# Conditioning units of a fused two-block kernel moved behind the expert loop, with a new order in its router stage

## What is computed

```python
def ada_modulation(c, w, b):
    m = jax.nn.silu(c) @ w + b                       # [1024] @ [1024, 3072]
    shift, scale, gate = jnp.split(m[:, None, :], 3, axis=-1)
    return shift, scale, 1.0 + gate

def moe_ffn(h, w_router, b_router, w_gate_up, b_gate_up, w_down, b_down):
    logits = hf @ w_router + b_router                # top 4 of 32 experts
    ...                                              # rows of a token's experts
        gu = xb @ w_gate_up[e] + b_gate_up[e]        # 1024 -> 2048
        glu = gate * jax.nn.sigmoid(SWIGLU_ALPHA * gate)
        return ((up + 1.0) * glu) @ w_down[e] + b_down[e]

def second_block(x, c, ...):
    for layer in range(2):
        shift, scale, gate = ada_modulation(c, ada_w[layer, 0], ada_b[layer, 0])
        y = mixer_ab(x * (1.0 + scale) + shift, ...)   # layer 0; mixer_c in layer 1
        x = layer_norm(DN_ALPHA * x + gate * y, ...)
        shift, scale, gate = ada_modulation(c, ada_w[layer, 1], ada_b[layer, 1])
        y = squared_relu_mlp(x * (1.0 + scale) + shift, ...)
        x = layer_norm(DN_ALPHA * x + gate * y, ...)
```

## Time and profile before

| | us |
|---|---|
| median of 3 runs | 1933.98 (1928.10 to 1935.94) |
| profiled execution | 1928.87, span 1927.0 |
| TensorE busy | 1826.0 (95%), mean granted clock 0.977 |
| DVE busy | 694.6 (36%) |
| ACT busy | 539.6 (28%) |
| input projection of the mixer starts | 89.14 |
| output projection of the mixer starts | 171.80 |
| logits done | 294.17 |
| first expert's bias matmuls start | 323.96 |
| last expert's down matmuls end | 1260.92 |
| scores of the ab attention start | 1328.72 |

### The profile page before, as it was taken

The page is one execution under the profiler, slowest core; times in us unless marked ns, Lnnn a source line. Parts: engine busy times, 40 slices in busy tenths (PEclk is TensorE's granted clock), DMA queues, the critical chain, the costliest instruction groups (busy, mean ns, idle before and its releaser), DMA issues.

```text
span 1927.0 us, 24801 instructions
## 1 busy us (share of the span) xinstructions
PE 1826.0 (95%) x10198; PEld 1129.0 (59%) x10198; DVE 694.6 (36%) x1177; ACT 539.6 (28%) x714; POOL 34.3 (2%) x21
## 2 busy tenths in 40 slices
PE   6999989999999999999999999996899999989997
PEld 6785764443434434434434434464589987769996
DVE  3243322111111111111111111158865568676545
ACT  4342431101111111111111111045634454464442
POOL 0100120000000000000000000000000000000001
PEclk9998998999999999999999999997799999999999
DMA  9758599999999999999999999913144553424550
GB/s 337 285 197 329 187 380 398 428 428 429 428 428 429 429 429 428 429 428 429 428 428 429 429 429 428 418 59 119 32 165 175 190 213 142 175 103 143 202 197 34
DMA packets 96315, 587.14 MB, mean 305 GB/s; under 512 B 6990, under 2 KB 7204, under 8 KB 70660
## 3 DMA queue, kind: packets, MB, share of 16 engines
q1 hardware_dynamic: 94820, 581.25, 74.6%
q10 hardware_dynamic: 1440, 5.11, 0.8%
HBM read 585.30 MB, written 1.05 MB: 304 GB/s over the span
## 4 chain that ended last, share of the span: by engine, by line
PE 88%; DVE 4%; ACT 4%; DMA 3%; issue 1%; SPq 0%; DVEq 0%; ACTq 0%
PE bank L1063 34%; PE bank L1319 23%; PE bank L1338 12%; PE bank L1276 7%; PE bank L1348 3%; PE bank L1310 2%; DMA ring<-in_ada_w 1%; PE bank L1138 1%; ACT arena L811 1%; PE bank L1331 1%; PE bank L1123 1%; ACT sb_XN L896 1%; DMA ring<-in_w_o 1%; PE bank L1255 0%; DMA ring<-in_w_in 0%
## 5 line engine op out<-in xcount | busy, mean ns | idle before, releaser
L1319 PE MATMUL bank<-ring,arena 128*64 128x512 f32 x2048 | 454.7, 596 | 0.0
L1319 PEld LDWEIGHTS bank<-ring,arena 128*64 128x64 f32 x2048 | 141.6, 137 | 307.4 <-issue 307.4
L1063 PE MATMUL bank<-w_hi,arena_r 128*128 128x512 f32 (+1 forms) x784 | 258.0, 391 | 4.7 <-DVE arena_r L2027 2.8
L1338 PE MATMUL bank<-ring,arena 128*64 128x512 f32 x1024 | 226.8, 595 | 16.8 <-ACT arena L811 16.8
L502 DVE TENSOR_TENSOR w_lo<-ring,w_hi 128x4096 fp32r<-128x4096 f32 (+2 forms) x45 | 196.5, 4367 | 47.3 <-ACT w_hi L492 44.9
L1063 PEld LDWEIGHTS bank<-w_hi,arena_r 128*128 128x128 f32 x784 | 148.0, 189 | 35.4 <-DVE arena_r L2027 3.3
L492 ACT ACTIVATE w_hi<-ring 128x4096 fp32r<-128x4096 f32 (+2 forms) x45 | 158.9, 3574 | 34.9 <-DMA ring<-in_c_w_in 19.2
L809 ACT ACTIVATE arena<-arena,sb_tab 128x512 f32<-128x512 f32 x32 | 23.1, 722 | 510.5 <-DVE arena L1930 510.5
L1338 PEld LDWEIGHTS bank<-ring,arena 128*64 128x64 f32 x1024 | 72.5, 137 | 150.5 <-issue 144.9
L1905 DVE TENSOR_SCALAR arena<-sb_tab,sb_pos 128x64 f32<-128x64 f32 x66 | 13.8, 252 | 387.7 <-PE bank L1319 387.7
L1063 PE MATMUL bank<-XT_r,w_hi 128*128 128x256 f32 x512 | 145.8, 285 | 4.3 <-DVE arena_r L2148 4.3
(11 more groups left out here) (341 smaller groups left out, 2120.3 us busy)
## 6 DMA issues: line engine op xcount, KB each, us to landing
ring<-in_w_gate_up SPq DMA_DIRECT2D x128, 2048.0 KB, 14.4
ring<-in_w_down SPq DMA_DIRECT2D x64, 2048.0 KB, 16.7
ring<-in_mlp_w SPq DMA_DIRECT2D x32, 2048.0 KB, 8.3
ring<-in_ada_w SPq DMA_DIRECT2D x24, 2048.0 KB, 12.5
ring<-in_c_w_in SPq DMA_DIRECT2D x6, 2048.0 KB, 7.6
ring<-in_w_in SPq DMA_DIRECT2D x4, 2048.0 KB, 10.0
ring<-in_w_k SPq DMA_DIRECT2D x2, 2048.0 KB, 12.2
ring<-in_w_v SPq DMA_DIRECT2D x2, 2048.0 KB, 9.1
```

Source lines behind the costliest of these rows:

```text
L1063: mm = pe.matmul(out, st[a], mv[b], start=start and a + b == 0, stop=stop and a == 1, skip_group_check=True)
L1319: mm = pe.matmul(B[m][CAP * h:CAP * h + CAP, :], xe[:, 2 * j + kl, :], w[:, kl, m * D + h * HW:m * D + (h + 1) * HW], start=False, stop=(j ...
L1338: mm = pe.matmul(B[2][CAP * h:CAP * h + CAP, :], hT[:, c, CAP * j:CAP * j + CAP], w[:, c, h * HW:(h + 1) * HW], start=(j == 0 and c == 0), ...
```

## The change

The first three sublayers' conditioning (18 units) stays ahead of the experts: 2, 4, 2, 1, 5 and 4 units in the six places, for 2, 3, 6, 1, 5 and 7. The six units of the fourth sublayer (`late`) come through `POST` as three granules of two transfers each, between ab_in 2 and ab_out 0, with the query weights behind the first. TensorE does two of them in place of the five `keep_busy` matmuls, one between two groups of transposes, three in the first steps of the ab attention, where their combines go too. The split of ab_out 1 moves from ahead of aqT's copy into the attention. In the router stage the first gather stands ahead of the table, and DVE does `gains_xe` ahead of it. In the loop the last eighth of the gather comes behind `hidden_T`. DVE writes the normalised rows in a reordered layout, so that the gather reads contiguous columns. POOL makes the fourth sublayer's gains from the late result.

```diff
-ADA_AT = [("k", 2, (0, 1), 2), ("v", 3, (0, 1), 2), ("mix", 6, (4, 5, 4, 5, 4, 3), 2), ("q", 1, (4,), 6), ("scores", 5, (5, 4), 6),
-          ("router", 7, (1, 2), 4)]
+LATE = 18
+ADA_AT = [("k", 2, (0, 1), 2), ("v", 4, (0, 1), 2), ("mix", 2, (4, 3), 2), ("q", 1, (4,), 6), ("scores", 5, (5, 4), 6),
+          ("router", 4, (1, 2), 4)]
...
-AHEAD = {("ada", 18): (0, 1), ("ada", 20): (2, 3)}
+AHEAD = {("ada", 15): (0, 1), ("ada", 17): (2, 3)}
...
-POST = ([("ab_in", i) for i in range(3)] + [("uq", 0)] + [("ab_out", i) for i in range(2)] + [("mlp0", i) for i in range(16)]
+POST = ([("ab_in", i) for i in range(3)] + [("late", 0), ("uq", 0), ("late", 1), ("late", 2)]
+        + [("ab_out", i) for i in range(2)] + [("mlp0", i) for i in range(16)]
...
+        def late_part(u):
+
+            if u in (LATE, LATE + 3, LATE + 5):
+                return [vec[:].rearrange("p a n -> p (a n)"), wr[:].rearrange("p k n -> p (k n)")]
+            at = 1224 if u == LATE + 4 else 9216
+            return [arn(at, S), arn(at + S, S)]
...
+            if name == "late":
+                out = []
+                for s2, u in ((s, LATE + 2 * i), (HI_SLOTS[POST_SLOTS.index(s)], LATE + 2 * i + 1)):
+                    w = A["ada_w_2"][u // 12, u // 6 % 2].rearrange("(k p) n -> p k n", p=P)
+                    out.append((slot(s2).rearrange("p (k n) -> p k n", k=8), w[:, :, HW * (u % 6):HW * (u % 6) + HW]))
+                return out
...
                 sp.wait_ge(used, NPRE if OWNER[g] is None else OWNER[g] + 1)
+                if name == "late" and g < MOE_END + R2:
+                    sp.wait_ge(used, MOE_END)
...
+            last = mod[:, 3, :]
+            pool.wait_ge(sem("late_read"), 2)
+            pool.tensor_tensor(last, last, ada_bT[:, 72:96], ALU.add).then_inc(sem("late_mod"), 1)
...
+            def late(u, b):
+
+                n = u - LATE
+                if n % 2:
+                    act.wait_ge(*done("late", n // 2))
+                else:
+                    act.wait_ge(sem("late_mm"), n // 2 + 1)
+                for i, part in enumerate(late_part(u)):
+                    act.activation(part, B[b][:, i * S:(i + 1) * S], ACT.Copy).then_inc(sem("late_part"), 1)
...
                 for u in range(units):
+                    if st == "ab" and u < 3:
+                        if u == 2:
+                            act.wait_ge(sem("late_comb"), 4)
+                        late(LATE + 3 + u, 7)
+                    if st == "ab" and u == 1:
+                        split_hi(act, "ab_out", 1)
...
+            late(LATE, 7)
+            late(LATE + 1, 6)
+            act.wait_ge(sem("late_comb"), 2)
+            act.activation(mod[:, 3, 0:8], B[7][:, 0:8], ACT.Copy).then_inc(sem("late_read"), 1)
             split_hi(act, "ab_out", 0)
-            split_hi(act, "ab_out", 1)
...
+            late(LATE + 2, 2)
             act.wait_ge(sem("ab_T"), 5)
...
-            def gather():
+            def gather(a=0, b=KC):
 
-                for k in range(KC):
+                for k in range(a, b):
                     for t in range(TB):
-                        rows = XN[:, t, 2 * P * (k // 2):2 * P * (k // 2 + 1)].rearrange("p (q r) -> p r q", r=2)
-                        mm = pe.matmul(B[3][:, k * CAP:(k + 1) * CAP], rows[:, k % 2, :], sel_tok[:, t, :],
+                        mm = pe.matmul(B[3][:, k * CAP:(k + 1) * CAP], XN[:, t, k * P:(k + 1) * P], sel_tok[:, t, :],
                                        start=(t == 0), stop=(t == 1))
-                mm.then_inc(sem("e_gather"), 1)
+                if b == KC:
+                    mm.then_inc(sem("e_gather"), 1)
 
-            ada(2)
+            ada(1)
...
-            ada(2)
+            ada(1)
+            pe.wait_ge(*upto("ffn", "xn", 2))
+            pe.wait_ge(sem("e_sel"), 2)
+            gather()
             pe.wait_ge(sem("flag"), 1)
...
-            pe.wait_ge(*upto("ffn", "xn", 2))
-            pe.wait_ge(sem("e_sel"), 2)
-            gather()
-            ada(1)
             ada_flush()
...
                 pe.wait_ge(sem("e_sel"), i * (2 * E_BLOCK) + (2 * n + 4))
-                gather()
+                gather(0, KC - 1)
                 pe.wait_ge(sem("e_h"), i * E_BLOCK + (n + 1))
                 hidden_T()
+                gather(KC - 1)
...
+            def late_step(u):
+
+                if u == 1:
+                    late_raw.extend(late_granule())
+                if u:
+                    pe.wait_ge(*upto("ab", "pte", 2 * u))
+                late_combine(LATE + 2 + u, 5, 400 + 4 * u)
+                if u < 3:
+                    late_main(LATE + 3 + u, late_raw[u], 7)
...
                         scores(st, u + 2, q, k)
+                    if st == "ab" and u < 4:
+                        late_step(u)
                     pe.wait_ge(*upto(st, "p", 2 * u + 2))
...
+            def late_main(u, raw, b):
+
+                w = raw.rearrange("p (k n) -> p k n", k=KC)
+                for r in range(2):
+                    for c in range(4):
+                        mm = pe.matmul(B[b][32 * c:32 * c + 32, :], cs[:, 2 * c + r, :], w[:, 2 * c + r, :],
+                                       start=(r == 0), stop=(r == 1))
+                mm.then_inc(used if (u - LATE) % 2 else sem("late_mm"), 1)
+
+            def late_combine(u, b, at_col):
+
+                pe.wait_ge(sem("late_part"), 2 * (u - LATE) + 2)
+                for i, part in enumerate(late_part(u)):
+                    for c in range(2):
+                        col_at = at_col + 2 * i + c
+                        mm = pe.matmul(B[b][:, col_at:col_at + 1], part[:, c * P:(c + 1) * P], quads[:, 0:1],
+                                       start=True, stop=True)
+                mm.then_inc(sem("late_comb"), 1)
...
-            keep_busy(7, 5)
+            late0 = late_granule()
+            late_main(LATE, late0[0], 7)
+            late_main(LATE + 1, late0[1], 6)
+            pe.wait_ge(sem("late_part"), 4)
...
             mm.then_inc(sem("ab_T"), 1)
+            late_combine(LATE, 7, 0)
+            late_combine(LATE + 1, 7, 4)
...
+            late1 = late_granule()
             for m, (st, src, e) in enumerate((("i_", R4b, 2), ("b_", R1b, 5))):
+                if m:
+                    late_main(LATE + 2, late1[0], 2)
...
+                    out, x = dst[:, t, :], src[:, t, :]
+                    if st == "ffn":
+                        out = out.rearrange("p (j r q) -> p j r q", r=2, q=P)
+                        x = x.rearrange("p (j q r) -> p j r q", r=2, q=P)
+                    dve.tensor_scalar(out, x, stat[:, 64 + at + t:65 + at + t], None, ALU.mult).then_inc(sem("xn"), 1)
...
+            dve.wait_ge(sem("gain_landed"), 16)
+            dve.wait_ge(sem("e_gather"), 1)
+            gains_xe()
             dve.wait_ge(sem("rank"), 1)
```

More of the change, by code:

```diff
@@ L138 @@
 X_SLOTS = E_SLOTS[2:4] + E_SLOTS[6:8]
-UQ = POST.index(("uq", 0))
+DOUBLE = [q for q, (name, _) in enumerate(POST) if name in ("late", "uq")]
 def slot_of(g):
@@ L167, in split_no @@
     q = g - MOE_END
-    assert q >= 0 and q != UQ
-    return 2 * len(SPLIT) + q + 1 - (q > UQ)
+    assert q >= 0 and q not in DOUBLE
+    return 2 * len(SPLIT) + q + 1 - sum(d < q for d in DOUBLE)
 NORMS = ("mem", "mix", "xa", "ffn", "fin")
@@ L601, in _ @@
             g = MOE_END
-            for name, count in (("ab_in", 3), ("uq", 1), ("ab_out", 2), ("mlp0", 16), ("c_in", 6), ("c_out", 2),
-                                ("mlp1", 16)):
+            for name, i in POST:
                 if name[:3] != "mlp":
-                    for i in range(count):
-                        if (name, i) not in POST[0:2]:
-                            post_fill(name, i)
-                        g += 1
+                    if (name, i) not in POST[0:2]:
+                        post_fill(name, i)
+                    g += 1
+                    continue
+                if i:
                     continue
@@ L860, in evac_hi @@
                 act.wait_ge(sem("mod_g"), 4)
+                if a == 3:
+                    act.wait_ge(sem("late_mod"), 4)
                 for q in range(4):
@@ L1466, in attend, with late_granule @@
                 outputs(units - 1)
+            def late_main(u, raw, b):
[13 more added lines that the diff above has]
+                mm.then_inc(sem("late_comb"), 1)
+            def late_granule():
+                g = at[0]
+                raw = granule()
+                return raw, slot(HI_SLOTS[(g - MOE_END) % R2])
             def split_granule():
```

41 lines of the change are left out of this document (25 added, 16 removed).

## The result

The changed kernel takes 1918.62 us (median of 7 runs, 1913.11 to 1921.59), the kernel before 1935.94 us (7 runs, 1928.1 to 1938.52). The ratio is 0.9912 with a 95% interval of 0.9891 to 0.9933: 0.9% or 17 us faster, inside the range on record (1897 to 1926) and 8.6 us above the forecast of 1910. The profiled execution of the changed kernel took 1920.11 us (span 1918.3), near its median; the profiled one of before, 1928.87, lies at the low end of its runs. So the two traces differ by 8.7 us only, where the medians differ by 17 and the forecast's sum was 21.7.

What follows compares the result with a forecast made beforehand. TensorE was taken to bound the expert loop, barely ahead of the DMAs. Terms +15.5 - 20.4 - 13.4 - 1.5 - 14.4 + 11.5 - 2 + 3 = -21.7 gave 1907.2 from 1928.87; forecast 1910 us between two bases, range 1897 to 1926.

Steps and rivals of the forecast that it cites:

- the 1.5 for the first expert's bias and gate matmuls: Loop's first expert: bias and gate matmuls no longer below full clock, 0.5 and 1.0 us, together -1.5.
- The term of 14.4: Expert loop: the gather's last eighth behind the hidden rows' transposes saves 0.45 us in each of 32 experts, -14.4.
- a margin of 4 to 6 us: Expert loop: DMA landings stay ahead of TensorE by 5.9 us, some 2 less for the fourth gate granule; TensorE barely stays the bound.
- loads into an idle DMA at the loop's end: Behind the loop: late 0's load meets idle DMAs; no cost to the ab_in projection, 0 us.
- Forecast -13.4: Router stage, four units for seven and gather first: first bias matmul at 310.5 for 323.96 us.
- with no idle that loss goes: Router stage: TensorE no longer idles for landings, so the first bias and gate matmuls' clock loss goes, -1.5 us.
- +15.5: Values stage: w_in's projection starts 13.8 us later by w_in 0's late slot and more units, plus 1 to 2 for half clock.
- -20.4: Mixer stage, two units for six: output projection waits for two units and one combine, 4.7 us, instead of 25.1.
- ab_out 0's wait: Behind the loop: ab_out 0 lands behind the late granules, ACT's split delays aqT's copies; scores at 1340.2 for 1328.72, +11.5 us.
- the rival in which ab_out 0 lands among the late granules: Behind the loop: ab_out 0 doesn't hold ACT up, -11.5 us, total 1899; chance 0.13.
- The other term, +3: Attention: three mains, four combines and ab_out 1's split partly hidden in waits; bounds -2 to +9, taken as +3 us.
- The rival on the slower side: Behind the loop: six late units find no wait, 5.4 us each at half clock, total about 1940; chance 0.11.

Runs made afterwards that it cites:

- the profile with the fast router stage: Profile of the changed kernel with ab_out 0 issued ahead of late 2's two transfers; 1909.67 us, ratio 0.9868 to the kernel before.
- before with the loop's part alone: Kernel before, with only the loop's gather split (seven eighths ahead of the transposes, one behind) and XN's rows contiguous; 1921.64 us, ratio 0.9916.
- The run with three units each: Changed kernel with three units in the values stage and three in the mixer stage, for 4 and 2; 1897.49 us, ratio 0.9798 to the kernel before.
- The run with narrow units: Changed kernel with the six late units multiplying 64 of their 512 columns only; 1917.67 us, ratio 0.9901 to the kernel before.
- both repairs: Changed kernel with three units each in values and mixer stages, and ab_out 0 issued ahead of late 2; 1888.99 us, again 1889.92 us.

## Why the prediction was right, and where it was not

**What bounds the kernel.** Right: both limits of the loop lie together, and TensorE's ended last. The experts gained 18.6 us for the 14.4 forecast; the 1.5 for the first expert's bias and gate matmuls didn't come in this profile (6.25 us for 6.24, both partly at half clock; 4.60 in the profile with the fast router stage). The term of 14.4 was mis-sized in two parts: the split gave 11.5 us, 0.36 per expert for 0.45, and the contiguous rows, which I had put at nothing, 7.0, 0.22 per expert. I had taken 122 against 118 ns a record as no difference; times 32 records and 32 experts that is 4 us, and measured it was 0.19 us per gather, 6 us.

**Can the DMAs follow?** In the sum this was a yes or no with a margin of 4 to 6 us. The margin was used up: the last landings took 32 to 35 us for the forecast 28, TensorE waited 0.5 us in one profile and 2.6 in the one with the fast router stage. I had counted the margin only for the loop's own matmuls. What stands behind the loop in the same queue, ab_in, was late by the same amount, landing 31 to 32 us after its issue for 15 to 16 before. It was still in flight when TensorE needed its own code, and cost 2.5 us by that. For the same reason a gain ahead of the loop isn't kept in full: with 9.2 us less at the first bias matmul (311.55 for 320.75), the ab_in projection came 7.2 us earlier (1252.76 for 1259.94).

**Loop's end to the ab_in projection.** The step that failed is the sentence that late 0 "loads into an idle DMA at the loop's end", costed at nothing. It delayed the code of TensorE itself, and behind the gap the clock-keeping matmuls ran at half clock: 3.7 us, given back when late 0 went out 11 us after the loop's end.

**Router stage.** Forecast -13.4, in the two traces -4.4. The working holds at full clock: 15.0 us from logits to bias in the changed code against 29.72, which is -14.7 (the sum had counted the first unit at the 3.32 us of the earlier trace rows; at full clock it takes 1.85). What failed is the sentence "with no idle that loss goes". TensorE had no idle time there and was at half clock for 20 us. The row of before was one execution too: before with the loop's part alone has the same order there and took 35.69 us, with less clock and as much waiting for landings. So the reordering is worth 4 to 21 us by the profiles one takes, and no pair of them is at one clock throughout.

**Values and mixer.** Values: +19.3 for +15.5, and the size that failed is the clock's. The part's copy ended at 93.66 (forecast 95.1 on a start 1.65 later, so to the point); from there two units and four combines took 12.9 us, to 106.55, where 1.85 a unit and 0.98 a combine make 7.6. I had 1 to 2 us for that half clock, it was 5. Mixer: -19.0 for -20.4. Their sum, +0.3 for -4.9, is why the stages bring nothing. The run with three units each shows that this loss was the price of one slot, not of moving units.

**Behind the loop.** ab_out 0's wait was forecast step by step, aqT 9.8 us late against the end of the ab_in projection's stretch; it was 9.6, and the rival in which ab_out 0 lands among the late granules fell. Unit 20's matmuls cost 3.6 as said. Scores to output projection was -5.1 for +1. Of this 3.2 is the scores at full clock: from the first of them to DVE's first step on the index scores it is 4.16 us for 7.39, where the sum had -2. The other term, +3, had the wrong sign, -1.9. What the sum feared did happen. The steps in the attention aren't hidden; the chain of the changed kernel goes through a combine and a unit at half clock

```profile
1334.84 1.79 PE bank L1545 x8
1336.63 3.57 PE bank L1535 x16
```

and through ACT's split of ab_out 1 (3.51 us) ahead of a copy. But with this work the rest of the attention ran at a higher clock (0.95 from 1337 to the output projection, 0.68 in the same part of before), and that gave back more. The run with narrow units shows that it is the late matmuls themselves that go with the higher clock.

**The rival on the slower side**, the units exposed at 5.4 us each, didn't occur: made narrow, they changed nothing in the total.

**To the end.** 547.4 us for 544.5 in code that nobody touched. The kernels here show either 544.6 or 547.4 (one 545.8), without relation to their edits. It comes in two steps of 1.3 to 1.6 us in the MLPs, and both are the clock: the changed kernel's profile has 0.72 from 1400 to 1406 us and 0.66 from 1725 to 1730, the profile before has 1.00 in the same two places of its work (1409 to 1415 and 1734 to 1740). Why the clock fell there isn't shown.

So the forecast was right in its range partly by luck. The experts gained 4 us more and the attention 6, while the values stage (4), the loop's end (6), the end (3) and the clock of the router stage (9 at half clock, none at full) took back more. The two traces differ by 8.7 us where the sum had 21.7; that the medians differ by 17 is also due to the profiled execution of before, which was a fast one.

## What to carry to other kernels

Where a loop runs with both limits together, read the landing times at its start and end: if they grow, the queue behind the loop is late too, and part of what TensorE gains ahead of it is lost. Issue what an in-order engine needs next ahead of what it needs later, and don't start a large transfer at the moment when an engine leaves a loop: look for the packets of the instruction queue there. A term that rests on one profiled execution's clock needs the same stretch from a second one before it is taken for the order of the work.

## What the runs showed of the hardware that I had not expected

- TensorE busy 5.00 of 5.00 us stays at 0.50 of its clock for 20 us (295 to 315) in work of units, combines, small sums and the gather; the same code runs at 1.00 in another profile.
- With the late units' matmuls whole, the granted clock from the scores to the output projection is 0.89, with an eighth of their columns 0.69; the stretch takes 48.7 and 54.2 us.
- The instruction queue's packets wait behind data: the first one behind the loop ended 3.8 us after the loop's end with nothing else in flight, 6.4 to 8.9 us with transfers in flight, and TensorE went on 1.42 to 1.44 us after it.
- In the gather a record took 122 ns with the stationary operand read at every second column and 116 ns with contiguous columns, 0.19 us of 3.91.
- The DMAs moved 428 GB/s on average over 900 us (330 to 1230), before and after, whatever the landing time (11 to 35 us).

Not tried: both repairs with late 0 issued later. It would save some 3 us more, an estimate: from the loop's end to the ab_in projection it takes 20.8 to 21.5 us with both repairs, and 18.1 in the kernel before with the loop's part alone, which had ab_in in flight but no late 0.
